# Depthwise convolution cut into single tiles, its sample part moved from GpSimd to VectorE

## The reference, cut to what matters

```
h = rmsnorm(x) modulated by c;  u = h @ w_in          # q, k, v, ca, cg of 512 columns each
q, k = per-head rmsnorm;  glu = ca * sigmoid(cg)
att = stick_breaking(q, k, v)                          # 8 heads x 64: sigmoids, a running product, a weighing, @ v
y[n, ch] = sum_tap glu_ext[n + tap, ch] * w[tap, ch] + b[ch]   # depthwise, causal, 31 taps, 512 channels
cv = silu(layernorm(y))
x = x + gate * (concat(att, cv) @ w_out);  then a mixture of 16 experts, two for each token
```

## Time and profile before

| | us |
|---|---|
| median of three runs | 1175.37 (1175.29 to 1179.02) |
| the profiled execution, own time | 1175.17 |
| its span, first to last instruction | 1173.4 |
| busy: PE | 1124.7 |
| busy: DVE | 641.4 |
| busy: ACT | 355.6 |
| busy: POOL | 254.6 |

### The profile page before, as it was taken

How to read it: one execution, slowest core, us unless ns; L and a number is a source line. 1 busy time by engine, 2 the same in 40 slices (tenths; PEclk the granted TensorE clock), 3 DMA queues, 4 the chain that set the end, 5 groups by cost and what they waited for, 6 DMA issues and landing times.

```text
span 1173.4 us, 19641 instructions
## 1 busy us (share of the span) xinstructions
PE 1124.7 (96%) x6700; PEld 542.7 (46%) x6700; DVE 641.4 (55%) x1271; ACT 355.6 (30%) x738; POOL 254.6 (22%) x305
## 2 busy tenths in 40 slices
PE   6899999999997989999999999999999999999996
PEld 4444444444445666666544444533333333333333
DVE  0010777877889999998985573832223223223222
ACT  2132221222128879898312222110110110110110
POOL 2011202220229910000010010123323323322322
PEclk9999999999999999999999999999999999999998
DMA  9942332133337565555523356699967697877983
GB/s 369 353 138 108 127 125 99 55 99 108 112 90 277 172 205 184 200 183 177 200 90 108 108 173 230 231 373 335 325 218 285 220 347 266 321 244 265 311 311 114
DMA packets 122630, 242.14 MB, mean 206 GB/s; under 512 B 17406, under 2 KB 31870, under 8 KB 121528
## 3 DMA queue, kind: packets, MB, share of 16 engines
q1 hardware_dynamic: 101729, 206.85, 50.2%
q0 software_dynamic: 16848, 29.66, 7.3%
q10 hardware_dynamic: 3984, 4.72, 1.2%
HBM read 371.46 MB, written 38.17 MB: 349 GB/s over the span
## 4 chain that ended last, share of the span: by engine, by line
PE 73%; DVE 9%; issue 5%; DMA 5%; ACT 5%; POOL 1%; SPq 1%; POOLq 0%; DVEq 0%; ACTq 0%
PE bank L2066 19%; PE bank L1648 19%; PE bank L2079 10%; PE bank L1847 7%; PE bank L1628 2%; PE bank L1711 2%; ACT mid L1270 1%; DVE cvT L2253 1%; PE bank L1683 1%; PE bank L2056 1%; DMA mid<-in_w_ada_dram 1%; DMA h_d<-low 1%; ACT big L1237 1%; PE bank L1766 1%; PE bank L1508 1%
## 5 line engine op out<-in xcount | busy, mean ns | idle before, releaser
L2066 PE MATMUL bank<-big,mid 128*64 128x512 f32 x1104 | 247.3, 594 | 0.0
L1648 PE MATMUL bank<-big 128*128 128x512 f32 x560 | 244.5, 594 | 0.1
L1648 PEld LDWEIGHTS bank<-big 128*128 128x128 f32 x560 | 104.8, 190 | 128.1 <-issue 128.1
L2253 DVE SCALAR_TENSOR_TENSOR cvT<-low,cw,cvT 128x256 f32<-128x256 f32 x360 | 156.4, 509 | 0.0
L2066 PEld LDWEIGHTS bank<-big,mid 128*64 128x64 f32 x1104 | 79.4, 137 | 151.3 <-issue 151.3
L2079 PE MATMUL bank<-big,mid 128*64 128x512 f32 x544 | 119.6, 592 | 0.0
L2362 DVE TENSOR_TENSOR_SCAN big<-big 128x513 f32<-128x513 f32 (+4 forms) x96 | 92.5, 1003 | 1.0 <-ACT big L1237 0.3
L1457 ACT ACTIVATE mid<-bank 128x512 f32<-128x512 f32 x17 | 10.2, 597 | 267.7 <-PE bank L2072 267.7
L915 POOL TENSOR_TENSOR st<-st,mhalf 128x16 f32<-128x16 f32 (+1 forms) x9 | 25.2, 2802 | 245.3 <-DVE st L2285 236.2
L2079 PEld LDWEIGHTS bank<-big,mid 128*64 128x64 f32 x544 | 39.1, 137 | 77.7 <-issue 77.7
L2968 DVE TENSOR_TENSOR mid<-bank,low 128x512 f32<-128x512 f32 x34 | 21.9, 685 | 95.9 <-PE bank L2079 95.9
(11 more groups left out here) (461 smaller groups left out, 1432.8 us busy)
## 6 DMA issues: line engine op xcount, KB each, us to landing
big<-in_w_gate_dram SPq DMA_DIRECT2D x74, 1024.0 KB
big<-in_w_up_dram SPq DMA_DIRECT2D x72, 1024.0 KB
big<-in_w_down_dram SPq DMA_DIRECT2D x72, 1024.0 KB
low<-in_w_ada_dram SPq DMA_DIRECT2D x32, 512.0 KB, 6.2
low<-in_cache_v_dram SPq DMA_DIRECT2D x64, 256.0 KB
big<-in_w_in_dram SPq DMA_DIRECT2D x8, 1280.0 KB, 17.3
mid<-in_w_ada_dram SPq DMA_DIRECT2D x8, 1024.0 KB, 13.5
xt<-in_x_prompt_dram SPq DMA_DIRECT2D x16, 512.0 KB, 5.9
```

Of the source, the lines that this page charges most:

```text
L1648: mm = pe.matmul(bank[:, 4 if cc == 2 else cc, :], hT[:, s, k, :], w_in_sb[:, k, cc * 512:(cc + 1) * 512], start=(k == 0), stop=(k == KD - 1))
L2066: mm = pe.matmul(bank[half, 2 * s + w, :], xgT[:, s, k, half], held[x][:, k, :], start=(k == 0), stop=(k == KD - 1))
L2253: c.put(V.scalar_tensor_tensor(out, src, cw[:, ch, tap:tap + 1], out, ALU.mult, ALU.add))
```

## The change

The prompt's convolution in the projection no longer goes by pairs and two channel groups but by `(first tile, tiles, first tap, last tap)` over all four channel groups, partly over single tiles (128 columns). Tile 6's taps 0 to 17 are done in the projection and in the seam; tile 7's taps 0 to 17 stand alone in attention, and from tap 18 on both tiles are done together. `TAPS_BY` is a table: 1 tap in cycle 0, none in cycles 1 to 4, then 2, 3, 2, 3, 2, 3, 2, 2, 2, 2, 2. The sample's convolution leaves POOL: DVE does it in cycles 1 to 4, one of the 4 new token positions in each, as one multiplication of 4 x 8 x 31 elements and one reduction over the taps, and a last addition of the bias. POOL waits for that (`smp_conv`) before `ln_sum`. The products lie in `mods`, so the first of them waits until the modulation rows that lay there are stored.

```diff
@@ pool
             pool.wait_ge(S["glu_sb"], NT)
             pool.wait_ge(S["mm_chunk"], MM_ALL)
-            c.put(pool.tensor_tensor(y_smp, glu_s[:, :, :, 0:DS], per_channel(0), ALU.mult))
-            for tap in range(1, CW):
-                c.put(pool.tensor_tensor(t_smp, glu_s[:, :, :, tap:tap + DS], per_channel(tap), ALU.mult))
-                c.wait()
-                c.put(pool.tensor_tensor(y_smp, y_smp, t_smp, ALU.add))
-                c.wait()
-            c.put(pool.tensor_tensor(y_smp, y_smp, per_channel(CW), ALU.add))
...
-            c.wait()
+            pool.wait_ge(S["smp_conv"], 1)
             ln_sum(0)
             ln_sum(2)
             ln_root(0)
@@ vector, projection
-            def conv_taps(pair, chs, t0, t1):
-                n0 = pair * 2 * P
+            def conv_taps(first, tiles, t0, t1):
+                n0, n = first * P, tiles * P
                 if t0 == 0:
-                    dve.wait_ge(S["glu_sb"], 2 * pair + 2)
+                    dve.wait_ge(S["glu_sb"], first + tiles)
                 for tap in range(t0, t1):
-                    for ch in chs:
-                        out = cvT[:, ch, n0:n0 + 2 * P]
-                        src = glu_x[:, ch, n0 + tap:n0 + tap + 2 * P]
+                    for ch in range(NCH):
+                        out = cvT[:, ch, n0:n0 + n]
+                        src = glu_x[:, ch, n0 + tap:n0 + tap + n]
...
-                            c.wait(back=len(chs) - 1)
+                            c.wait(back=NCH - 1)
...
+            CONV_PARTS = {(2, 0): [(0, 2, 0, 6)], (2, 1): [(0, 2, 6, 8)], (2, 2): [(0, 2, 8, 19)],
+                          (3, 0): [(0, 2, 19, 26)], (3, 1): [(0, 2, 26, 28)], (3, 2): [(0, 2, 28, CW), (2, 1, 0, 12)],
+                          (4, 0): [(3, 1, 0, 9)], (4, 1): [(3, 1, 9, 12)], (4, 2): [(2, 2, 12, 23)],
+                          (5, 0): [(2, 2, 23, 30)], (5, 1): [(2, 2, 30, CW)], (5, 2): [(4, 1, 0, 17)],
+                          (6, 0): [(5, 1, 0, 10)], (6, 1): [(5, 1, 10, 13)], (6, 2): [(5, 1, 13, 17), (4, 2, 17, 25)],
+                          (7, 0): [(4, 2, 25, CW), (6, 1, 0, 2)], (7, 1): [], (7, 2): [(6, 1, 2, 14)]}
+            AHEAD = 18
...
-                    chs = (0, 1) if j % 2 == 0 else (2, 3)
-                    cuts = (0, 16, 20, CW) if t < NTP - 1 else (0, 22, 24, LATE_TAP)
-                    conv_taps(j // 2, chs, cuts[part], cuts[part + 1])
+                for first, tiles, t0, t1 in CONV_PARTS.get((t, part), ()):
+                    conv_taps(first, tiles, t0, t1)
...
-            conv_taps(NTP // 2 - 2, (2, 3), LATE_TAP, CW)
+            conv_taps(NTP - 2, 1, 14, AHEAD)
@@ vector, attention
-                n0 = SEQ - 2 * P
+                n0 = SEQ - P if tap < AHEAD else SEQ - 2 * P
...
+            def conv_sample(n):
+                if n == 0:
+                    dve.wait_ge(S["glu_sb"], NT)
+                    for stored in rows_stored:
+                        dve.wait_ge(stored, 8 * NLATE)
+                c.put(V.tensor_tensor(weighed, glu_s[:, :, :, n:n + CW],
+                                      cw[:, :, 0:CW].unsqueeze(2).broadcast_to([P, NCH, DB, CW]), ALU.mult))
+                c.wait()
+                c.put(V.tensor_reduce(y_smp[:, :, :, n], weighed, AX_X, ALU.add))
+                c.wait()
+                if n == DS - 1:
+                    V.tensor_tensor(y_smp, y_smp, cw[:, :, CW:CW + 1].unsqueeze(3).broadcast_to([P, NCH, DB, DS]),
+                                    ALU.add).then_inc(S["smp_conv"], 1)
+
-            TAPS_BY = [max(cy, min(2 * cy - 4, CYCLES + cy - 6)) for cy in range(CYCLES + 1)]
+            TAPS_BY = (0, 1, 1, 1, 1, 1, 3, 6, 8, 11, 13, 16, 18, 20, 22, 24, CW - 5)
...
+                if cy in SMP_AT:                       # (1, 2, 3, 4)
+                    conv_sample(SMP_AT.index(cy))
                 for tap in range(TAPS_BY[cy], TAPS_BY[cy + 1]):
                     conv_tap(tap)
```

More of the change, by code:

```diff
@@ L2251, in conv_taps @@
                         else:
-                            c.wait(back=len(chs) - 1)
+                            c.wait(back=NCH - 1)
                             c.put(V.scalar_tensor_tensor(out, src, cw[:, ch, tap:tap + 1], out, ALU.mult, ALU.add))
-            LATE_TAP = 26
-            def conv_part(t, part):
-                j = t - 2
-                if 0 <= j < NTP - 2:
-                    if j == 0 and part == 0:
-                        dve.wait_ge(S["st_sb"], 1 + 2 * NCH)
-                    chs = (0, 1) if j % 2 == 0 else (2, 3)
-                    cuts = (0, 16, 20, CW) if t < NTP - 1 else (0, 22, 24, LATE_TAP)
-                    conv_taps(j // 2, chs, cuts[part], cuts[part + 1])
+            CONV_PARTS = {(2, 0): [(0, 2, 0, 6)], (2, 1): [(0, 2, 6, 8)], (2, 2): [(0, 2, 8, 19)],
[5 more added lines that the diff above has]
+            AHEAD = 18
+            def conv_part(t, part):
+                if (t, part) == (2, 0):
+                    dve.wait_ge(S["st_sb"], 1 + 2 * NCH)
+                for first, tiles, t0, t1 in CONV_PARTS.get((t, part), ()):
+                    conv_taps(first, tiles, t0, t1)
             dve.wait_ge(S["pool_const"], 2)
@@ L2426, in ln_sum2 @@
                     .then_inc(S["ln_sum2"], 1)
-            TAPS_BY = [max(cy, min(2 * cy - 4, CYCLES + cy - 6)) for cy in range(CYCLES + 1)]
+            y_smp = cvT[:, :, SEQ:TOK].rearrange("p c (b n) -> p c b n", b=DB)
+            weighed = mods[:, 0:NCH * DB * CW].rearrange("p (c b k) -> p c b k", c=NCH, b=DB)
+            SMP_AT = (1, 2, 3, 4)
+            def conv_sample(n):
[12 more added lines that the diff above has]
+            TAPS_BY = (0, 1, 1, 1, 1, 1, 3, 6, 8, 11, 13, 16, 18, 20, 22, 24, CW - 5)
             assert TAPS_BY[-1] == CW - 5
```

6 lines of the change are left out of this document (1 added, 5 removed).

## The result

The changed kernel takes 1181.39 us (median of 6 runs, 1179.18 to 1182.8). The kernel before takes 1175.69 (6 runs). The ratio is 1.0046 with an interval of 1.0032 to 1.0061: slower by 0.46%, 5.4 us (the medians are 5.7 us apart). The forecast was 1179.7. The profiled execution took 1180.69 us.

A forecast was written before the change was run, and what follows sets the result against it. It took PE to bound projection and, with handovers to ACT, attention, and DVE the seam. Seam +6.5, cycles 0 to 5 -3.8 and cycle 15 +1.6 gave +4.3 on 1175.17, 1179.5, plus 0.2: 1179.7 us; own range 1177 to 1182.

The forecast's parts named there:

- rival C: Seam and cycle 5: clock drop costs 1.6 us, cycle 5 takes cycle 4's whole loss (+1.8); +7.7, 1183.1 us; chance 0.12.
- Price of a narrow tap: DVE's convolution: a 128-column tap takes 0.27 us, bounds 0.235 and 0.40, against 0.398 for a 256-column one.
- Rival D: DVE's convolution: a narrow tap costs nearly 0.40 us; +12.6, 1188 us; chance 0.05.
- Projection: Tiles 2 to 6: no change, DVE's work hidden by PE; in tile 7 L2281 starts 1.7 us earlier.
- The seam on DVE: Between projection and attention: 64 narrow taps for 18 wide ones, +10.1 us; first scan +8.1 us, at about 359.7.
- The seam on PE: PE up to cycle 1: 8.1 us late less 1.6 of slack, +6.5 us, bounds +4.3 and +14.8.
- Cycles 1 and 4: Attention: POOL's 61 operations and their stretching of DVE go, `ln_sum` moves; -2.0 and -4.0 us.
- Cycle 5: Attention: POOL's `ln_sum` now stretches scans and weighings here by 3.2 us, less slack and earlier start; +2.2 us.
- Cycles 6 to 13: Attention: no change, since PE sets these cycles; two or three narrow taps replace two wide ones.
- Rival B: Attention is bound by DVE, so cycles shorten by what DVE loses; -2.8, 1172.6 us, or 1168.3; chance 0.18.
- Cycle 15: End of attention: one more wide tap ahead of what PE already waits for; +1.6 us, wait about 1.9 us.
- Rival A: Seam cheaper with narrow taps at 0.235 (+4.3), cycle 5 takes LN sums for nothing; -0.1, about 1175.3 us; chance 0.20.

The follow-up runs named there:

- e12: Changed kernel with 3, 5 and 1 dummy matmuls filling PE's waits in the seam; 1183.65 us, ratio 1.0060 to the kernel before.
- e8: Changed kernel with 3 and 4 dummy matmuls in PE's two waits of the seam; 1182.42 us, ratio 1.0055 to the kernel before.
- e3: Changed kernel with the sample's convolution back on POOL and none on DVE; 1181.97 us, ratio 1.0052 to the kernel before.
- e10: e9 with the sample's convolution back on POOL and none on DVE; 1172.46 us, ratio 0.9971 to the kernel before.
- e9: Changed kernel with 32 narrow taps in the seam instead of 64, attention's taps redistributed, first `ln_sum` before POOL's wait; 1171.84 us, ratio 0.9961 to the kernel before.
- e4: Changed kernel with the taps of cycles 6 to 11 left out, for reading times alone; one time, 1186.12 us.
- e1: Changed kernel with all 64 narrow taps taken out of the seam and their work given to attention; 1174.08 us, ratio 0.9983 to the kernel before.

## Why the prediction came out as it did

The forecast of 1179.7 was 1.7 us below the median, inside its own range of 1177 to 1182. The direction came from the right place. The number owes something to luck: the seam was taken too low by 2.65 us and cycle 5 too high by 1.1, and 1181.39 lies as near to rival C's 1183.1 as to the forecast. Step by step:

- **Price of a narrow tap: right.** 0.27 us was forecast; 16 in a row take 4.16, 0.26 each, and 12 in a cycle of attention take 3.23. Rival D (0.40) is out. The table row that the Trainium skill gives in "VectorE: DVE Perf Modes", section on the TRN2 errata, worked out to 0.19; the trace says 0.26, as for the wide tap it says 0.398 against 0.33. The section says itself that this row comes out too low for the time of a single instruction, which the prediction left out.
- **Projection: right.** The long part of tile 6 takes 19.05 us (forecast 19.2), the gating of tile 7 starts at 316.50, and PE waits for nobody from 60 to 336 us. L2271 starts at 330.42, right after its squares (329.36 + 1.02). Against zero that is 1.71 us sooner than before, as forecast.
- **The seam on DVE: right.** The 48 taps take 14.81 us (15.2 forecast). The first scan is 7.65 us later against zero, where 8.1 was forecast, and stands at 358.73 against 359.7.
- **The seam on PE: the term that was mis-sized.** +6.5 was forecast, up to cycle 1; it was +9.15. Two parts. L1565 is later by 7.14 us against zero, since POOL's scaled q and k (L923) starts 7.84 later and took 1.57 us in place of 0.72, 0.85 more; of these 8.7 the slack behind it takes 1.55. And from there to cycle 1 2.0 us were lost to the half clock, which the sum had at nothing. The prediction had it as rival C at 1.6 us and gave that a chance of 0.12. It took its mechanism from cycle 4 of the kernel before, where a wait of 2.0 us came with a clock of 0.89, and named the wait of about 4 us ahead of the late variance. By its own sum for the seam that wait is twice as long, and so the clock belonged into the forecast. The size is about right (e12), the place is not: the clock fell before that wait began, after the 3.14 us that PE waited for the sample's gating (L2302), a wait that the prediction doesn't name. With that one filled (e8) it stayed up there and fell later.
- **Cycles 1 and 4: right in size, the reason right in part.** -2.2 and -4.0 against -2.0 and -4.0. I had put the gain down to POOL's 61 operations, the stretching that they cause, and `ln_sum`'s move. For cycle 4 that is wrong: e3 and e10 have POOL's work there and take 12.72 and 12.90 us, so it is the missing tap of cycle 3. For cycle 1 it holds with a light seam, where POOL's absence brings 2.3 us (e9 against e10) and the missing tap nothing (14.67 in e10, 14.62 before). In the kernel after it brings 0.5; the other 1.7 come with the long cycle 0, in which DVE catches up, and are a part of the seam's loss given back.
- **Cycle 5: too much.** +2.2 was forecast and 1.1 measured. The scans take 2.83 and the weighings 2.10 us in place of 1.8 and 1.0. That is 2.1 us of stretching where 3.2 were put down, since these are pairs of 384 columns and not of 512, and DVE had more slack too (the 1.36 us ahead of them). PE waited 1.5 us for L2378, and no half clock followed. This error and that of the seam have opposite signs. The price of the sample's convolution was right: 1.19 us for the multiplication and 1.19 for the reduction, 2.4 a cycle as forecast.
- **Cycles 6 to 13: right.** 13.30, 12.71, 12.64 and 12.47 us as before, and e4 shows why. Rival B fell with it. (Two or three narrow taps are 2.2 to 3.2 us by the prediction's own price, not 0.8 to 3.2 as it says; nothing hangs on it.)
- **Cycle 15: right.** The wait before L1862 is 1.84 us (1.9 forecast), and against zero `mix` loses 1.6 to it.
- **Rival A** failed in the seam, where it had put a narrow tap at 0.235 and no clock; in cycle 5 it was 1.1 us too low.

By steps: +9.15 - 2.2 - 4.0 + 1.1 + 1.6 = +5.6, where the forecast had +4.3. So rival C was true in one of its two places: in the seam with 2.0 us (1.6 forecast), in cycle 5 not at all (1.8 forecast).

## What to carry over

An engine that isn't the bound still has stretches where it is: here DVE is busy for 56% of the span and yet sets the seam, because in its order the taps stand ahead of what PE waits for. Size such filler by the wait that it is to fill, read in the trace (DVE's 4.6 and 4.3 us in e1), and not by an even share of the work: with 32 narrow tap instructions in the seam cycle 1 started 0.2 us later than before, with 64 it started 9.15 us later. Where a release moves, look at what stands next in the other engine's order: POOL's `ln_sum` cost nothing in cycle 4 where DVE had no tap ahead of it (e3), 1.1 us beside the scans of cycle 5, and 4 to 5 beside a tap. An edit that gains in one cycle can lose the same in the next. And read a gain against a run that has the loss removed: in e3 cycle 1 looked cured, and in e10 its wait was back.
